# Even mixer on Trainium2: the RMS factor applied to the in-projection's outputs instead of its inputs

## The reference, cut to what matters

```python
def rms_norm(x, g):
    y = xf * lax.rsqrt(jnp.mean(xf * xf, axis=-1, keepdims=True) + RMS_EPS)
    return (y * g.astype(jnp.float32)).astype(x.dtype)

def modulate(x, g, shift, scale):
    return rms_norm(x, g) * (1 + scale) + shift

def even_mixer(h, w_in, w_out, ...):          # h = modulate(x, ...)
    q, k, v, a = jnp.split(h @ w_in, [ATT_Q, ATT_Q + ATT_KV, ATT_Q + 2 * ATT_KV], axis=-1)
    q = rms_norm(q.reshape(bsz, length, N_HEADS, HEAD_DIM), q_g)
    k = rms_norm(k.reshape(bsz, length, N_KV_HEADS, HEAD_DIM), k_g)
    ...                                       # rotary, softmax attention
    glu = a[..., :CONV_CH] * jax.nn.sigmoid(a[..., CONV_CH:])
    conv = jax.nn.silu(layer_norm(depthwise_conv(glu, conv_w, conv_b), cn_g, cn_b))
    return jnp.concatenate([attn, conv], axis=-1) @ w_out, own_kv
```

## Time and profile before

| what | value |
|---|---|
| median of 3 runs | 1394.48 us (1393.17 to 1394.87) |
| profiled execution, first to last instruction | 1392.1 us |
| its own total time | not given apart from the span |
| PE busy | 1375.7 us, 99% |
| DVE busy | 969.9 us, 70% |
| ACT busy | 553.6 us, 40% |
| POOL busy | 47.9 us, 3% |
| mean granted PE clock | 0.995 |
| 16 quad transfers (L474), median from issue to landing | 2.5 us |
| even mixer, in-projection to out-projection | 308.3 to 457.8 us |

### The profile page before, as it was taken

The page is one execution under the profiler, slowest core; times in us unless marked ns, Lnnn a source line. Parts: engine busy times, 40 slices in busy tenths (PEclk is TensorE's granted clock), DMA queues, the critical chain, the costliest instruction groups (busy, mean ns, idle before and its releaser), DMA issues.

```text
span 1392.1 us, 21240 instructions
## 1 busy us (share of the span) xinstructions
PE 1375.7 (99%) x8125; PEld 1340.9 (96%) x8125; DVE 969.9 (70%) x1472; ACT 553.6 (40%) x762; POOL 47.9 (3%) x50
## 2 busy tenths in 40 slices
PE   7999999999999999999999999999999999999999
PEld 6999999999949999999999999999999999999999
DVE  5688889949885888878238887797475488444422
ACT  4433333236476733333237333332365363333320
POOL 0000000011001200000001000000010100000000
PEclk8999999999999999999999999999999999999999
DMA  9766567533412466654334655674343253333331
GB/s 380 301 229 229 212 226 246 213 130 108 147 45 79 170 230 227 230 213 152 137 135 178 233 223 211 218 256 160 121 144 122 91 212 128 137 127 136 137 124 73
DMA packets 48759, 245.98 MB, mean 177 GB/s; under 512 B 6337, under 2 KB 10689, under 8 KB 28097
## 3 DMA queue, kind: packets, MB, share of 16 engines
q1 hardware_dynamic: 48416, 245.12, 48.5%
q10 hardware_dynamic: 288, 0.13, 0.0%
HBM read 241.12 MB, written 1.70 MB: 174 GB/s over the span
## 4 chain that ended last, share of the span: by engine, by line
PE 96%; DVE 2%; DMA 1%; ACT 1%; SPq 0%; issue 0%; DVEq 0%; ACTq 0%
PE ps L1388 30%; PE ps L1390 30%; PE ps L1389 30%; DMA m_raw<-in_w_pairs 1%; PE ps L1843 0%; PE ps L1449 0%; DVE conv L1157 0%; PE ps L1794 0%; PE ps L1795 0%; PE ps L1796 0%; PE ps L1723 0%; PE ps L1818 0%; PE ps L1465 0%; PE ps L1685 0%; PE ps L1697 0%; DVE smax L1228 0%
## 5 line engine op out<-in xcount | busy, mean ns | idle before, releaser
L1388 PE MATMUL ps<-a_hi,w_hi 128*128 128x384 f32 x1584 | 533.0, 337 | 0.5 <-DVE a_lo L965 0.3
L1389 PE MATMUL ps<-a_lo,w_hi 128*128 128x384 f32 x1584 | 530.0, 335 | 0.0
L1390 PE MATMUL ps<-a_hi,w_lo 128*128 128x384 f32 x1584 | 529.9, 335 | 0.0
L879 DVE TENSOR_TENSOR w_lo<-w_raw,w_hi 128x2048 fp32r<-128x2048 f32 x153 | 352.0, 2303 | 190.8 <-ACT w_hi L564 190.8
L564 ACT ACTIVATE w_hi<-w_raw 128x2048 fp32r<-128x2048 f32 x153 | 291.9, 1910 | 252.5 <-DMA w_raw<-in_w_units 252.4
L1388 PEld LDWEIGHTS ps<-a_hi,w_hi 128*128 128x128 f32 x1584 | 297.9, 188 | 6.7 <-issue 3.4
L901 DVE SCALAR_TENSOR_TENSOR m_raw<-m_raw 128x1024 f32<-128x1024 f32 x256 | 299.2, 1218 | 0.0
L1389 PEld LDWEIGHTS ps<-a_lo,w_hi 128*128 128x128 f32 x1584 | 298.0, 188 | 0.1
L1390 PEld LDWEIGHTS ps<-a_hi,w_lo 128*128 128x128 f32 x1584 | 297.9, 188 | 0.0
L1390 PE MATMUL ps<-h_hi,w_lo 128*128 (+1 forms) x704 | 235.1, 334 | 0.0
L1388 PE MATMUL ps<-h_hi,w_hi 128*128 (+1 forms) x704 | 235.1, 334 | 0.0
(11 more groups left out here) (193 smaller groups left out, 832.2 us busy)
## 6 DMA issues: line engine op xcount, KB each, us to landing
w_raw<-in_w_units SPq DMA_DIRECT2D x153, 1024.0 KB, 4.9
m_raw<-in_w_rows SPq DMA_DIRECT2D x128, 512.0 KB, 5.6
m_raw<-in_w_pairs SPq DMA_DIRECT2D x5, 1024.0 KB, 13.7
p_raw<-in_w_pairs SPq DMA_DIRECT2D x3, 1024.0 KB, 24.8
m_raw<-padded SPq DMA_DIRECT2D x32, 53.4 KB, 2.5
x<-in_x_cols SPq DMA_DIRECT2D x2, 768.0 KB, 5.2
out<-x SPq DMA_DIRECT2D x8, 192.0 KB, 1.9
fourier<-in_k_fourier SPq DMA_DIRECT2D x1, 768.0 KB, 7.8
```

The source lines that it names most:

```text
L879: nc.vector.tensor_tensor(w_lo[:, slot(u), :], w_raw[:, slot(u), :], w_hi[:, slot(u), :].bitcast(FP32), ALU.subtract).then_inc(lo_done, 1)
L1388: mm(out, whi, mhi, start=start, stop=False)
L1389: mm(out, whi, mlo, start=False, stop=False)
L1390: return mm(out, wlo, mhi, start=False, stop=stop)
```

## The change

The even mixer starts like the others, and goes further: all seven input units run on x * scale, in a_hi and a_lo, which get 16 more columns for the purpose.

- `raw_pair(n)` lets the raw code write a_hi, a_lo for n = 1. `norm(1)` with its dummy matmuls, `first_unit`, `norm_sums` and PE's and DVE's `norm` go; PE runs `raw_units(u, 1)`, then u+2 to u+6 with 386 columns each.
- DVE gets `take(n)`, once per unit: wait for the unit and for n_rms, copy the four shift columns from PSUM (for Q and K also a copy times the norm's weight), multiply both banks, 128 x 768, by the root into qk or into prob / prob_t. PE now waits for take (in_scaled) where it waited for ACT or for glu_mul before it reuses a bank.
- ACT's `sigmoid` and `qkv_evict` wait for take, read SBUF, and work in two pieces (context, latent), since the shift is a per-group bias. `glu_mul` adds the shift to its first operand. V moves from v_raw to qk[QT + 1].
- Placement: DVE's glu_mul(0) moves from in front of split(u+3) to behind split(u+4); six taps of tile 0 move from before the rotary step to behind glu_mul(2), whose place is now behind split(u+8); of tile 2's taps four instead of seven stand before attention, and steps 3 to 5 get three instead of two. ACT splits u+2 and u+3 inside raw_norm. PE's sums for Q 2 and 3 move from row 3 to row 6 of u+4. Two waits on a_ready go (SP in front of the rope transfers, POOL in front of the memset). POOL adds seven squares instead of five.

```diff
@@ DVE
-            inverse_rms(1)
-            norm(1)
+            def take(n):
+                bank = IN_BANK[n]
+                dve.wait_ge(unit_done, RING + u + n + 1)
+                dve.wait_ge(rms_copied, 1)
+                shifts = ps[:, bank:bank + 2, TOK:TOK + 2]
+                nc.vector.tensor_copy(in_shift[:, n], shifts)
+                if n in QKV_UNITS:
+                    col = B_KG if n == 1 else B_QG
+                    nc.vector.tensor_scalar(in_shift_g[:, n - 1], shifts, vec_b[:, col:col + 1], None, ALU.mult)
+                    dst = qk[:, (QT, 0, 2)[n - 1]:(QT, 0, 2)[n - 1] + 2, :]
+                else:
+                    dst = glu_pair(GLU_UNIT.index(n))[:]
+                nc.vector.tensor_tensor(dst, ps[:, bank:bank + 2, 0:TOK], n_rms[:].unsqueeze(1).to_broadcast([P, 2, TOK]),
+                                        ALU.mult).then_inc(in_scaled, 1)
...
             split(u + 2)
-            glu_mul(0)
             split(u + 3)
             dve.wait_ge(vectors_in, 48)
+            take(0)
+            take(1)
+            split(u + 4)
+            glu_mul(0)
             dve.wait_ge(glu_done, 1)
             taps(0, 0, 5)
-            split(u + 4)
-            taps(0, 5, 16)
+            take(2)
             split(u + 5)
-            taps(0, 16, 24)
+            taps(0, 5, 13)
+            take(3)
             split(u + 6)
-            taps(0, 24, 28)
+            taps(0, 13, 20)
...
-            taps(0, 28, 30)
+            taps(0, 20, 23)
...
-            taps(0, 30, CONV_K)
+            taps(0, 23, 25)
+            take(4)
             split(u + 7)
             glu_mul(1)
...
             nc.vector.tensor_tensor(qk[:, QT, :], qk[:, QT, :], ps[:, BC_BANK_K, 0:TOK], ALU.mult).then_inc(k_roped, 1)
+            take(5)
+            split(u + 8)
             glu_mul(2)
+            taps(0, 25, CONV_K)
...
-            split(u + 8)
             dve.wait_ge(glu_done, 3)
-            taps(2, 0, 7)
+            taps(2, 0, 4)
+            take(6)
             glu_mul(3)
...
-                k = 7 + 2 * m + min(m, 3)
-                taps(2, min(k, CONV_K), min(k + 2 + (m < 3), CONV_K))
+                k = 4 + 2 * m + min(m, 6)
+                taps(2, min(k, CONV_K), min(k + 2 + (m < 6), CONV_K))
@@ PE
-            norm(1)
             u = UNIT0[1]
-            first_unit(u, GLU_BANK[0], 1)
-            in_unit(u + 1, QKV_BANK[1])
-            in_unit(u + 2, QKV_BANK[2])
+            raw_units(u, 1)
+            in_unit(u + 2, IN_BANK[2], cols=TOK + 2)
...
+            pe.wait_ge(in_scaled, 1)
             qk_sums(QT)
             cached_and_values()
-            pe.wait_ge(glu_done, 1)
-            in_unit(u + 3, QKV_BANK[3])
+            in_unit(u + 3, IN_BANK[3], cols=TOK + 2)
             qk_sums(0)
             qk_sums(1)
-            in_unit(u + 4, GLU_BANK[1], 0, {3: last_sums})
-            in_unit(u + 5, GLU_BANK[2], 0, {3: spread_keys})
+            pe.wait_ge(in_scaled, 2)
+            in_unit(u + 4, IN_BANK[4], 0, {6: last_sums}, cols=TOK + 2)
+            pe.wait_ge(in_scaled, 3)
+            in_unit(u + 5, IN_BANK[5], 0, {3: spread_keys}, cols=TOK + 2)
             pe.wait_ge(k_roped, 1)
-            pe.wait_ge(glu_done, 2)
+            pe.wait_ge(in_scaled, 5)
@@ ACT
-            norm_stats(1)
-            norm(1)
+            raw_norm(1, UNIT0[1])
...
-                act.wait_ge(unit_done, RING + u + n + 1)
+                act.wait_ge(in_scaled, n + 1)
...
-            split(u + 2)
-            split(u + 3)
             sigmoid(0, 0)
             split(u + 4)
             qkv_evict(1)
@@ constants
-GLU_BANK = [0, 2, 4, 6]
-QKV_BANK = {1: 2, 2: 4, 3: 0}
+IN_BANK = [0, 2, 4, 0, 2, 4, 6]
```

More of the change, by code:

```diff
@@ L344, in build, with raw_pair, glu_pair @@
         block = ctx.enter_context(nc.Block())
+        def raw_pair(n):
+            return (a_hi, a_lo) if n == 1 else (xt_hi, xt_lo)
+        def glu_pair(j):
+            return prob_t if j % 2 else prob
         def slot(u):
@@ L507, in add_squares @@
             def add_squares(n):
-                for d in range(1, ADDED if n == 1 else KT):
+                for d in range(1, KT):
                     pool.wait_ge(sq_done, KT * n + d + 1)
@@ L568, in preload, with first_stats @@
                 nc.scalar.activation(warm[:, n:n + 1], ones[:, 0:1], func)
-            def norm_stats(n):
-                preload(n, ACT.Sqrt)
+            def first_stats():
+                preload(0, ACT.Sqrt)
                 for d in range(KT):
[L573 to L582, removed]
+                    act.wait_ge(x_ready, d + 1)
+                    nc.scalar.activation(n_sq[:, d, :], x[:, d, :], ACT.Square).then_inc(sq_done, 1)
+                act.wait_ge(stat_done, 1)
                 nc.scalar.activation(stat[:, 4:4 + TT], ps[:, 0, 0:TT], ACT.Sqrt, scale=1.0 / D_MODEL,
@@ L697, in qkv_evict @@
             def qkv_evict(n):
[L699 removed]
+                act.wait_ge(in_scaled, n + 1)
                 for h in range(2):
[L701 to L711, removed]
[L713 to L714 removed]
+                    tile = (QT, QT + 1, 0, 1, 2, 3)[2 * (n - 1) + h]
+                    if tile <= QT:
+                        for cnd, lo, hi in SEGS:
+                            ins = nc.scalar.activation(qk_sq[:, tile, lo:hi], qk[:, tile, lo:hi], ACT.Square,
+                                                       bias=in_shift[:, n, h, cnd:cnd + 1])
+                        ins.then_inc(qk_sq_done, 1)
+                    col = B_KG if tile == QT else B_QG
+                    for cnd, lo, hi in SEGS:
+                        if tile > QT:
+                            ins = nc.scalar.activation(qk[:, tile, lo:hi], qk[:, tile, lo:hi], ACT.Identity,
+                                                       bias=in_shift[:, n, h, cnd:cnd + 1])
+                        else:
+                            ins = nc.scalar.activation(qk[:, tile, lo:hi], qk[:, tile, lo:hi], ACT.Identity,
+                                                       bias=in_shift_g[:, n - 1, h, cnd:cnd + 1], scale=vec_b[:, col:col + 1])
+                    ins.then_inc(qk_copied, 1)
             sigmoid(0, 0)
@@ L1559, in proj_out @@
                         ins = three(ps[:, d0 + d, 0:TOK], tile_of(w_hi, u, at), tile_of(w_lo, u, at),
-                                    a_hi[:, kt0 + k, :], a_lo[:, kt0 + k, :], not last and k == 0, last and k == 3)
+                                    a_hi[:, kt0 + k, 0:TOK], a_lo[:, kt0 + k, 0:TOK], not last and k == 0, last and k == 3)
                     if last:
@@ L1862 @@
 FOUR_BANK = [6, 7, 0, 1]
-GLU_BANK = [0, 2, 4, 6]
-QKV_BANK = {1: 2, 2: 4, 3: 0}
+IN_BANK = [0, 2, 4, 0, 2, 4, 6]
+GLU_UNIT, QKV_UNITS = [0, 4, 5, 6], (1, 2, 3)
 BC_BANK_K = 7
-ADDED = KT - 2
-SUMMED = [0, ADDED - 1] + [ADDED - 1 + (KT - 1) * n for n in range(1, 5)]
+NORMED = {0: 0, 2: 1, 3: 2, 4: 3, 5: 4}
+SUMMED = [(KT - 1) * n for n in range(N_SUB)]
 SUM_BANK_RAW, BC_BANK_RAW = 6, 7
```

144 lines of the change are left out of this document (63 added, 81 removed).

## The result

The changed kernel takes 1398.93 us (median of 5 runs, 1397.24 to 1400.0) where the kernel before takes 1393.17 in the same comparison: a ratio of 1.0039, with a 95% interval of 1.0028 to 1.0049. By that ratio it is slower by 5.4 us; the prediction said 1394.7, no change, counted from the 1394.48 of three runs of the kernel before. The profiled execution took 1397.88, its span is 1396.1.

What follows compares the result with a forecast made beforehand. TensorE, busy 99% of the span, was taken to bound the kernel. Attention's start (-0.5), the clock (+0.3) and taps (+0.4) made +0.2 us on 1394.48, so 1394.7; the 8-in-10 range was 1390.5 to 1397.8.

Steps and rivals of the forecast that it cites:

- The change touches one stretch: Scope: only first FFN's end (308.3 us) to second FFN's start (457.8) was costed; nothing was counted elsewhere.
- the 7.2 us at the border: First FFN to mixer: PE gets past unit u+2's start at 326.55 instead of 333.8, 7.2 us sooner.
- The load came no sooner: Weights of u+4 in the mixer: their slot frees no earlier, so ACT's split starts at 330.55, DVE's at 332.6.
- 0.4 was taken for the taps: Attention steps 3 to 5: three more taps on DVE cost 0.4 us, range 0 to 1.4.
- Attention starts 0.5 us sooner: Mixer's end: sigmoid and glu_mul(3) done at 380.9 against 381.4 before, a gain of 0.5 us.
- the term of 0.3 for the clock: PE's clock, with PE idle 3.7 us before the rotated keys: a cost of 0.3 us, range 0 to 0.3.
- All at nothing: The mixer's other waits and GpSimd's added squares were covered: cost 0, under 1 us each if a cover is gone.
- (c): Rival: slower, because the half clock after the wait for the keys lasts into attention; chance 0.11.
- (a): Rival: PE's 3.5 us lead at the first scores carries through attention, 1391.0; chance 0.15, full form (1387.8) 0.03.
- (b): Rival: the takes are hidden and nothing moves, within a few tenths of 1394.5; chance counted in the main case.
- the main case: Whole kernel: 1394.7 us, no change, range of its own 1393.2 to 1396.7; chance 0.69.
- (d): Rival: the border's wait stays because xt_low is late, about as slow as no change; chance 0.02.

Runs made afterwards that it cites:

- before_pitch400: The kernel before with a_hi and a_lo at 400 columns a tile instead of 384, nothing else changed: 1397.01 us, ratio 1.0026.
- p400_all_hold: v384_all_hold with a_hi and a_lo put back to 400 columns a tile in every stage: 1395.59 us, ratio 1.0014 to the kernel before.
- before_pitch416: The kernel before with 416 columns (1664 bytes) a tile in a_hi and a_lo: 1403.15 us, one execution.
- after_view384: The changed kernel with a_hi and a_lo back at 384 columns a tile everywhere but in the even mixer's input: ratio 1.0020 to the kernel before.
- after_pitch448: The changed kernel with 448 columns (1792 bytes) a tile in a_hi, a_lo, xt_hi and xt_lo: ratio 1.0026 to the kernel before.
- v384_fill_idle: after_view384 with ACT's key eviction, and DVE's glu_mul(0) and five taps, ahead of their splits of u+4: ratio 1.0002 to the kernel before.
- v384_all: after_view384 with the edits of v384_fill_idle and v384_hold_u5, and rope, ck_nat and v_nat loaded ahead of u+4: ratio 0.9997 to the kernel before.
- v384_key_hold: after_view384 with 14 unread matmuls ahead of PE's wait for the rotated keys: ratio 1.0007 to the kernel before.
- v384_all_hold: v384_all with unread matmuls ahead of the waits for the keys and the scores of steps 2, 4, 7 and 10: 1391.81 us, ratio 0.9988.
- before_shift64: The kernel before with 64 unused bytes behind x, so every tile lies 64 bytes further on: 1392.16 us, one execution.
- before_xt448: The kernel before with 448 instead of 400 columns a tile in xt_hi and xt_lo alone: ratio 1.0004.
- v384_hold_u5: after_view384 with the load of u+5 issued only when u+4's has landed: 1394.43 us, one execution.

## Why the prediction was wrong, step by step

**The step that failed** is in its first part: "The change touches one stretch, from the end of the first FFN (308.3 us) to the start of the second one (457.8)". The change also gives a_hi and a_lo another shape, 400 columns a tile in place of 384, and these two are the moving operand of 4752 matmuls, some 4400 of them outside the input units of the mixer. The prediction asked what was added, removed and moved, and never what address each matmul reads from: this term stood at nothing, without a reason. It is 3.6 us in two kernels (before_pitch400, p400_all_hold), of the 5.4 measured. The layouts tried in the kernel before differ by up to 10 us (before_pitch416, one execution).

**What held.** PE gains the 7.2 us at the border: the key sums behind u+2 start at 335.24 where 335.0 was predicted, with a border 0.26 later. take(1) costs 1.14 from its first copy at 327.28 to the end of its product, predicted 1.1. The load came no sooner: DVE idles 5.04 us in front of the split of u+4 (4.7). PE waits 3.74 us for the keys' factor (3.7), and the mean clock of 0.72 from 369 to 375 is 3.4 us at 0.50, 1.7 lost. From the first exp to the end of the last values it is 40.43 us against 40.12: 0.31, where 0.4 was taken for the taps.

**What was off by a little.** The split of u+4 starts 0.86 later than predicted and its load 0.96, which "no sooner than before" did not allow for. DVE's queue behind it, up to the end of the keys' factor, was 35.4 us where 35.5 was predicted, and so passed the delay on: the factor ends at 368.82 (368.1). take(6) starts at 379.26 (378.3 + 0.3 = 378.6), and the first exp at 382.55, against 382.21 before: 0.34 later, where "Attention starts 0.5 us sooner", less 0.3 for the clock, was predicted; 0.26 of that is the later border. In sum the mixer is 0.39 us longer in the profile, where -0.5 + 0.3 + 0.4 = +0.2 was predicted. No run shows the term of 0.3 for the clock as such; what the profile after shows in its place is one fall of 3.4 us at 0.50 behind the wait for the keys, and DVE waiting 0.33 for u+6 in front of take(6). "All at nothing" was true of the mixer's own waits in this profile (in after_view384, with the load 1.75 later, PE waits 0.62 in front of the key sums and 0.77 in front of the transposes behind them), but not of GpSimd's adds one border later, which PE waited 1.0 to 1.3 us for in three of the ten profiles with the new order (after, after_pitch448, v384_fill_idle), with a fall of the clock behind it in the last two.

**The rivals.** (c), with 4.9 us for a longer fall (3.5, which no run shows) and the taps (1.4), -0.5 + 4.9 = +4.4, stood at 1398.9, the measured time, and by luck: its mechanism isn't there, the clock is back at 1.00 from 375 on, and no fall shows in the attention of that profile. The falls of other executions are (c) in kind, at 3.4 us of 0.50 each, 1.7 us lost and not 3.5. (a) is against the trace: PE's scores start 1.03 us sooner and the exp waits for the sigmoid and for the table load behind it (1.28 us from 381.14), as argued; v384_all shows that even a lead of 4.2 us is spent in the attention. (b), nothing moves, is as wrong in the total as the main case, and for the mixer alone it can't be told from it. (d) is out: the first raw matmul starts at 308.54, right behind the FFN's last. In the trace the clock fell at 369 to 375, behind the wait of 3.74 us, and in v384_key_hold, where unread matmuls leave 0.64 of that wait, it did not. What is left of the 5.4 us beside the layout, some 2, holds the mixer's 0.4, the wait for GpSimd, and the clock; how it is shared among them these runs don't settle.

## What to carry to other kernels

A shape in a diff is a change to every instruction that reads the tensor (here 4752 matmuls, and 3.6 us): list them all, and take the cadence of the commonest before believing that a change is local. If one stage needs wider rows, give that stage its own view of the bytes and leave the others theirs. The drift that grew evenly here over stages that the change doesn't touch was a rate, not a wait, and two rows 96 matmuls apart showed it (16.64 us against 16.69 and 16.91). The lead won ahead of the loop between the engines was mostly spent in the loop's own waits: of 4.9 us at the first scores v384_all kept 0.4, and v384_all_hold, in which unread matmuls held the clock in those waits, kept 2.0.

## What the hardware did that was not expected

TensorE's matmuls of 384 fp32r columns follow each other after 173.33 ns with 1536 or 1792 bytes between the tiles that they read, 173.89 (176 where the tile changes every three matmuls) with 1600, and 175.0 (175.5) with 1664. All tiles 64 bytes further on: 173.33. With 386 columns the mean is 176.0 ns with 1600 bytes (176.3 in before_shift64) and 176.6 with 1792. Among waits of 0.7 to 1.6 us in the attention the clock fell to 0.50 for 3.4 us in some profiles and not in others whose mixer is the same (before_xt448, before_pitch400 and before_pitch416 have the fall, before and before_shift64 have none there). Behind the wait for the keys it fell in all five profiles with a wait of 2.1 us or more that nothing fills (in v384_hold_u5 from 0.4 us before the wait's end), and in neither of the two with 1.7.
